# A mixture of experts on one core: two more slots in the ring of weights, shorter routing, small last loads, combines in halves

## The reference, cut to what matters

```
g_logits = t @ rg_w + rg_b                 # 4 groups
g_w      = softmax(g_logits)[argmax]
e_logits = (t @ re_w + re_b) of that group # 8 experts in a group
top_v, top_i = top_k(e_logits, 2)
weights  = g_w * softmax(top_v)
y[token] = sum over its 2 experts e of
           weights[e] * ((silu(t @ wg[e]) * (t @ wu[e])) @ wd[e])   # hidden width 512
h = h + y
return rmsnorm(h, final_norm_w)
```

## Time and profile before

| | |
|---|---|
| median of three runs | 1322.72 us (1322.7 to 1324.62) |
| the profiled execution, its own time | 1325.48 us |
| its span, first to last instruction | 1323.6 us |
| TensorE busy | 1281.5 us (97%) |
| VectorE, ScalarE busy | 588.7 us (44%), 470.3 us (36%) |
| DMA | 349.35 MB |
| chain that ended last | TensorE 83%, VectorE 6%, DMA 6%, ScalarE 3% |
| TensorE clock granted | 0.996 of full speed |

### The profile page before, as it was taken

One profiled execution on the slowest core, in us unless ns is written; L12 is line 12 of the kernel. 1 busy time (PEld: TensorE's weight loads), 2 busy tenths in 40 slices (PEclk: granted clock), 3 DMA queues, 4 the chain that ended last, 5 costly groups with the idle time before them and its releaser, 6 DMA issues.

```text
span 1323.6 us, 19228 instructions
## 1 busy us (share of the span) xinstructions
PE 1281.5 (97%) x8372; PEld 969.0 (73%) x8372; DVE 588.7 (44%) x939; ACT 470.3 (36%) x698; POOL 64.8 (5%) x68
## 2 busy tenths in 40 slices
PE   8999999999999999999999999999999999999996
PEld 7887888999998889979999998834344343443432
DVE  3576656444556576595555566522011110111112
ACT  4543555434454644544654554311111010110102
POOL 4021000000001021010200000000000000000000
PEclk9999999999999999999999999999999999999999
DMA  9776336555543534443455559489999999999995
GB/s 354 276 279 241 149 128 236 181 189 191 174 157 111 185 128 159 148 163 128 107 170 179 176 187 379 165 358 420 421 419 421 421 421 421 420 421 421 421 421 210
DMA packets 102548, 349.35 MB, mean 264 GB/s; under 512 B 6114, under 2 KB 9472, under 8 KB 77888
## 3 DMA queue, kind: packets, MB, share of 16 engines
q1 hardware_dynamic: 100912, 345.56, 68.5%
q0 software_dynamic: 1376, 2.50, 0.8%
q10 hardware_dynamic: 176, 0.07, 0.0%
HBM read 347.05 MB, written 1.05 MB: 263 GB/s over the span
## 4 chain that ended last, share of the span: by engine, by line
PE 83%; DVE 6%; DMA 6%; ACT 3%; issue 1%; DVEq 0%; ACTq 0%
PE bank L553 43%; PE bank L939 14%; PE bank L974 7%; DMA weights<-in_expert_w_up 4%; PE bank L790 3%; PE bank L749 3%; PE bank L474 2%; DMA arena<-in_expert_w_up 2%; DVE WHL L1412 2%; PE bank L580 2%; PE bank L510 1%; ACT WHL L993 1%; PE bank L520 1%; PE bank L690 1%; PE bank L716 1%
## 5 line engine op out<-in xcount | busy, mean ns | idle before, releaser
L553 PE MATMUL bank<-XH,WHL 128*128 128x256 f32 x2928 | 541.2, 285 | 7.6 <-DVE WHL L1412 3.8
L553 PEld LDWEIGHTS bank<-XH,WHL 128*128 128x128 f32 x2928 | 462.6, 193 | 12.1 <-DVE WHL L1412 5.5
L553 PE MATMUL bank<-XL,WHL 128*128 128x256 f32 x1464 | 415.4, 284 | 0.0
L1412 DVE TENSOR_TENSOR WHL<-weights,WHL 128x1024 fp32r<-128x1024 f32 x223 | 282.7, 1284 | 211.8 <-ACT WHL L993 211.4
L993 ACT ACTIVATE WHL<-weights 128x1024 fp32r<-128x1024 f32 x223 | 231.9, 1054 | 213.5 <-PE bank L553 207.9
L553 PEld LDWEIGHTS bank<-XL,WHL 128*128 128x128 f32 x1464 | 282.7, 193 | 0.1
L939 PE MATMUL bank<-arena 128*64 128x512 f32 x512 | 142.2, 593 | 2.6 <-DMA arena<-in_expert_w_up 2.6
L939 PE MATMUL bank<-weights,arena 128*64 128x512 f32 x384 | 113.6, 593 | 5.2 <-DMA weights<-in_expert_w_up 5.1
L553 PE MATMUL bank<-WHL,XH 128*128 128x512 f32 x320 | 102.4, 394 | 4.1 <-DVE WHL L1412 4.1
L939 PEld LDWEIGHTS bank<-arena 128*64 128x64 f32 x512 | 45.3, 137 | 72.0 <-issue 67.1
L2113 DVE SCALAR_TENSOR_TENSOR chainm<-bank,small,chainm 128x512 f32<-128x512 f32 x16 | 12.0, 750 | 183.1 <-PE bank L939 183.1
(11 more groups left out here) (347 smaller groups left out, 1216.4 us busy)
## 6 DMA issues: line engine op xcount, KB each, us to landing
weights<-in_w_in SPq DMA_DIRECT2D x58, 1024.0 KB, 5.0
arena<-in_expert_w_gate SPq DMA_DIRECT2D x32, 1024.0 KB, 19.6
arena<-in_expert_w_up SPq DMA_DIRECT2D x32, 1024.0 KB, 22.8
arena<-in_expert_w_down SPq DMA_DIRECT2D x32, 1024.0 KB, 26.2
weights<-in_expert_w_up SPq DMA_DIRECT2D x24, 1024.0 KB, 24.7
weights<-in_expert_w_down SPq DMA_DIRECT2D x24, 1024.0 KB, 24.4
weights<-in_expert_w_gate SPq DMA_DIRECT2D x24, 1024.0 KB, 21.0
weights<-in_w_ada SPq DMA_DIRECT2D x22, 1024.0 KB, 7.4
```

The costliest lines, as they stand in the source:

```text
L553: ins = e.matmul(o, l, r, start=first, skip_group_check=True, stop=g.part == g.parts - 1 and k == g.kc - 1 and n == 2)
L1412: e.tensor_tensor(lo, unit_weights(g, u), hi, ALU.subtract).then_inc(S.w_lo, 1)
```

## The change

- **Ring of eighteen.** The arena gives nine slots instead of eight, eight of them at the ring's start. To make room, several small tensors leave the arena or share memory with others. An eighteenth slot is `hT`, the transposed rows, free when the logits are done.
- **One buffer in place of two** for `hp`, `hpT`, `yo` and `wpick`; their writers wait for the readers in the pair before. `wpT`, the turned weights, keeps two.
- **Routing.** The picks of the first two pairs come from one 1024-wide product (`direct`) and one sum. `inpair` is made after the first choosing. ScalarE copies the token rows once more in chunk order (`full`), and the subtraction for `ulo` reads that copy. 15 spins instead of 32.
- **Order in a pair.** `turn_weights` stands between gate and up from the second pair on. Half of the combine comes before the transposes, the other half after them (and after the choosing). In the last pair the whole combine of the pair before comes between gate and up.
- **Last loads.** The second down half of the last pair is loaded as four pieces of 512 KB in place of two of 1,024 KB. VectorE's copy of the output waits for 6 of 8 signals.
- **Last norm.** Its weight row is kept in three pieces (`frow`), loaded after the first block's final norm. The products for the second half of a row are two, and VectorE's order at the end is changed.
- Three semaphores are merged into others.

```
-        c32 = sb("c32", [P, KC, 32])
+        spare = sb("spare", [P, 3 * T])
...
-        assert b5.at <= ARENA - 8 * SLOT, b5.at
+        wpick = maskf[:, HID:HID + T].rearrange("p (j s) -> p j s", j=TT)
+        assert b5.at <= ARENA - 9 * SLOT, b5.at
+        frow = [spare[:, 0:512], spare[:, 512:768], maskf[:, 768:1024]]
...
-        hp = [chainm[:, i * HID:(i + 1) * HID] for i in range(2)]
-        hpT = [maskf[:, i * HID:(i + 1) * HID].rearrange("p (k s) -> p k s", k=4) for i in range(2)]
+        hp = chainm[:, 0:HID]
+        hpT = maskf[:, 0:HID].rearrange("p (k s) -> p k s", k=4)
...
+            def turn_weights(p):
+                clear(6)
+                w.wait_ge(S.m_slots, weighed(p))
+                for j in range(TT):
+                    ins = e.transpose(bank[6][:, j * P:(j + 1) * P], wpick[:, j, :], ident[:, :])
+                ins.then_inc(S.m_wt, 1)
+                free[6] = (S.m_wc, p + 1)
+
-            def combine(p):
+            def combine(p, parts=range(4)):
                 w.wait_ge(S.m_wc, p + 1)
-                for i in range(4):
+                for i in parts:
...
-            spin(7, 32)
+            spin(7, 15)
...
                     free[b] = (S.m_h2 if wi else S.m_h1, p + 1)
+                    if wi == 0 and p:
+                        turn_weights(p)
+                        if p == NPAIR - 1:
+                            combine(p - 1)
...
-                if p:
-                    combine(p - 1)
+                if p == 0:
+                    turn_weights(0)
+                elif p < NPAIR - 1:
+                    combine(p - 1, (0, 1))
                 clear(7)
                 w.wait_ge(S.m_h2, p + 1)
...
                     choose(p // 2 + 1)
+                if 0 < p < NPAIR - 1:
+                    combine(p - 1, (2, 3))
                 w.wait_ge(S.m_hc, p + 1)
...
-                            x = moe_load(p, 2, half, s_)
+                            alone = p == NPAIR - 1 and k == 3
+                            x = 12 * NPAIR + s_ if alone else moe_load(p, 2, half, s_)
...
+            for j in range(TT):
+                e.activation(by_chunk(full)[:, j, :, :], xtok2[:, j, :].rearrange("p (q k) -> p q k", k=KC),
+                             ACT.Copy).then_inc(S.rn, 1)
...
-                w.wait_ge(S.rn, j + 1)
-                e.tensor_tensor(ulo[:, j, :].rearrange("p (k q) -> p k q", k=KC),
-                                xtok2[:, j, :].rearrange("p (q k) -> p k q", k=KC),
-                                uhi[:, j, :].bitcast(F32).rearrange("p (k q) -> p k q", k=KC),
-                                ALU.subtract).then_inc(S.rl, 1)
+                w.wait_ge(S.rn, TT + j + 1)
+                e.tensor_tensor(ulo[:, j, :], full[:, j, :], uhi[:, j, :].bitcast(F32), ALU.subtract).then_inc(S.rl, 1)
...
-            then(e.tensor_tensor(inpair, ph.unsqueeze(2).broadcast_to([P, two, 2, CAP]),
-                                 par.unsqueeze(3).broadcast_to([P, two, 2, CAP]), ALU.mult))
+            then(e.tensor_tensor(direct, ph.unsqueeze(2).broadcast_to([P, two, 4, CAP]),
+                                 dv[:, :, 0:4].unsqueeze(3).broadcast_to([P, two, 4, CAP]), ALU.mult))
             last()
-            for p in range(2):
-                slots_of(p, pick[:, :, p * P:(p + 1) * P], pair)
+            by_rank = direct.rearrange("p (j r) e s -> p j r (e s)", r=2)
+            e.tensor_tensor(pick[:, :, :], by_rank[:, :, 0, :], by_rank[:, :, 1, :], ALU.add).then_inc(S.m_slots, 1)
...
-                w.wait_ge(S.m_dn, 8 * p + 8)
-                if p >= 2:
-                    w.wait_ge(S.m_cb, 4 * (p - 1))
-                e.tensor_copy(yo[p % 2][0], bank[6][:, :]).then_inc(S.m_yv, 1)
+                w.wait_ge(S.m_dn, 8 * p + 6)
+                if p:
+                    w.wait_ge(S.m_cb, 4 * p)
+                e.tensor_copy(yo[0], bank[6][:, :]).then_inc(S.m_yv, 1)
...
+            w.wait_ge(S.fin, KC)
+            for f_, (c0, c1) in zip(frow, FROW):
+                e.dma_start(f_, a["norm_final_w_2"][c0:c1].rearrange("(o e) -> o e", o=1).partition_broadcast(P).rearrange(
+                    "p o e -> p (o e)")).then_inc(S.d_late, 16)
...
+                            if x >= 12 * NPAIR - 2:
+                                e.dma_start(moe_weights(x, 2, D)[:, 0, :], src[:, 2, :]).then_inc(moe_landed(x)[0], 16)
...
+            for s_ in range(2):
+                x = 12 * NPAIR + s_
+                w.wait_ge(*moe_released(x - len(moe_ring)))
+                e.dma_start(moe_weights(x, 2, D)[:, 0, :],
+                            a["expert_w_down_2"][0, NE - 2 + s_].rearrange("(p k) n -> p k n", p=P)[:, 3, :]).then_inc(
+                                moe_landed(x)[0], 16)
...
-        moe_ring = arena_ring[0:7] + [(base_slots[:, (nload + i) % RING, :], s_slot[(nload + i) % RING], None,
+        moe_ring = arena_ring[0:8] + [(base_slots[:, (nload + i) % RING, :], s_slot[(nload + i) % RING], None,
                                        (nload + i) % RING) for i in range(RING)]
-        moe_ring += arena_ring[7:] + [(late[:, i, :], sem(f"late_slot{i}_loaded"), (S.mm, len(units)), None) for i in range(2)]
+        moe_ring += arena_ring[8:] + [(late[:, i, :], sem(f"late_slot{i}_loaded"), (S.mm, len(units)), None) for i in range(2)]
+        moe_ring += [(hT[:, :, :].rearrange("p k t -> p (k t)"), sem("h_slot_loaded"), (S.lg, TT), None)]
```

More of the change, by code:

```diff
@@ L252, in build @@
         w8 = b5.take([P, KC])
-        frow = b5.take([P, D])
         tri = b5.take([P, P])
@@ L259, in build @@
         ss = b5.take([P, 8])
-        wpT = [hT[:, i, :] for i in range(2)]
+        wpT = [chainm[:, HID + i * T:HID + (i + 1) * T] for i in range(2)]
         rt = b5.take([P, TT, 96])
@@ L275, in build @@
         wcol = b5.take([P, TT, 1])
-        wpick = [hT[:, 2 + i, :].rearrange("p (j s) -> p j s", j=TT) for i in range(2)]
-        yhalf = b5.take([P, 512])
-        assert b5.at <= ARENA - 8 * SLOT, b5.at
+        wpick = maskf[:, HID:HID + T].rearrange("p (j s) -> p j s", j=TT)
+        assert b5.at <= ARENA - 9 * SLOT, b5.at
+        frow = [spare[:, 0:512], spare[:, 512:768], maskf[:, 768:1024]]
+        FROW = [(0, 512), (512, 768), (768, 1024)]
         b6 = Region(2048)
@@ L868, in tensor @@
             weave([gemm(n) for n in ("gk", "gv0", "gv1", "rq0", "rq1", "rk0", "rk1")],
-                  (2, gated(GL, [(S.gb, 1), by["gk"].freed[1]], by["gv1"].freed[1])), (13, gated_spread(GL, S.oGn)))
+                  (2, gated(GL, [(S.hb, 2), by["gk"].freed[1]], by["gv1"].freed[1])), (13, gated_spread(GL, S.oGn)))
             weave([gemm(n) for n in ("rv0", "rv1", "rv2", "rv3", "gg0", "gg1", "ma0", "ma1")],
@@ L971, in tensor @@
                         for s_ in range(2):
[L972 removed]
+                            alone = p == NPAIR - 1 and k == 3
+                            x = 12 * NPAIR + s_ if alone else moe_load(p, 2, half, s_)
                             w.wait_ge(*moe_landed(x))
[L974 to L975 removed]
+                            ins = e.matmul(bank[6 + n][64 * s_:64 * s_ + 64, :], hpT[:, k, 64 * s_:64 * s_ + 64],
+                                           moe_weights(x, 2, D)[:, 0 if alone else kk, n * 512:(n + 1) * 512],
+                                           start=k == 0, stop=k == 3)
                             if kk == 1:
@@ L1927, in vector @@
             weave([gemm(n) for n in ("gk", "gv0", "gv1", "rq0", "rq1", "rk0", "rk1")],
-                  (-1, log_decay()), (2, gated(GL, [(S.gb, 1), by["gk"].freed[1]])))
+                  (-1, log_decay()), (2, gated(GL, [(S.hb, 2), by["gk"].freed[1]])))
             for i in range(2):
@@ L2051, in vector @@
             chosen(0)
+            then(e.tensor_tensor(inpair, ph.unsqueeze(2).broadcast_to([P, two, 2, CAP]),
+                                 par.unsqueeze(3).broadcast_to([P, two, 2, CAP]), ALU.mult))
             then(e.tensor_tensor(eg, gl, gmax.broadcast_to([P, TT, 4]), ALU.subtract))
@@ L2105, in vector @@
                     assert nslots[0] == picked(p // 2 + 1)
-                if p >= 2:
-                    w.wait_ge(S.m_wt, p - 1)
-                slots_of(p, wpick[p % 2], wpair)
+                if p:
+                    w.wait_ge(S.m_wt, p)
+                slots_of(p, wpick, wpair)
                 assert nslots[0] == weighed(p)
@@ L2141, in scaled @@
                 w.wait_ge(S.rstd, NORMS + j + 1)
-                for n in range(2):
-                    c = slice(n * 512, (n + 1) * 512)
-                    e.scalar_tensor_tensor(out=normed[:, j, c], in0=xtok2[:, j, c], scalar=sj, in1=frow[:, c],
-                                           op0=ALU.mult, op1=ALU.mult).then_inc(S.t_out, 1)
             added(0, 0)
@@ L2150, in vector @@
             added(1, 1)
-            scaled(0)
+            inverted(0)
+            times_row(0, 0)
             summed(1)
-            scaled(1)
+            times_row(0, 1)
+            inverted(1)
+            times_row(1, 0)
```

(1 more changed line is left out.)

96 lines of the change are left out of this document (49 added, 47 removed).

## The result

The changed kernel takes 1312.1 us (median of six runs, 1311.37 to 1313.87) against 1322.94 us for the kernel before on the same chip: a ratio of 0.9918, with a 95% interval of 0.9906 to 0.993, or 9.3 to 12.4 us. Forecast were 1311.1 us, 11.65 us off the median. A second group of five runs gave 1313.38 against 1323.34 us, 0.9923 (0.9909 to 0.9936). The profiled execution took 1312.08 us with a span of 1310.4.

What follows compares the result with a forecast made beforehand. The stream of expert loads bounds the stage, TensorE what lies before and behind it. Savings of 3.84 + 4.99 + 1.97 + 0.80 + 0.05 = 11.65 us give 1311.1 us, range 1308.6 to 1314.8 us.

Steps and rivals of the forecast that it cites:

- What bounds: Expert stage: loads bound it; the time L, when the last up load frees TensorE, comes 8.83 us sooner.
- Shorter routing: Before the first choosing: 15 spins instead of 32, with VectorE's picks and subtractions in time, bring everything behind 3.84 us sooner.
- Rival (b): Routing: VectorE sets it, picks or subtractions up to 1.8 us late; 1312.9 us, chance 0.12.
- Eighteen slots: Load ring: two more loads issued before the hole leave 174 instead of 176 in the stream, saving 4.99 us.
- Rival (d): Load ring: the two extra loads don't shorten the stream, as something else holds its start or end; 1316.1 us, chance 0.06.
- The last pair: Last pair of experts: turning and combine moved between gate and up; down starts 1.97 us sooner against L.
- The end: After the last down phase: the final combine no longer waits for the first output half's copy, saving 0.8 us.
- The last norm: Final norm on VectorE: products split, VectorE's wait for ScalarE's root now under a product; 0.05 us saved.
- Rival (e): Last four 512 KB loads land late, the last 8.6 us after it is wanted; 1319.7 us, chance 0.05.
- Rival (c): Last pair: TensorE's clock falls after standing still, costing about 1.7 us; 1312.8 us, chance 0.08.
- Other pairs: Ordinary pairs: halved combines make TensorE 5 us quicker in sum, which gives nothing while the loads bound.
- Rival (f): Ordinary pairs: waits from single buffers make TensorE the bound; 1333 us at 2 us a pair, chance 0.05.

Runs made afterwards that it cites:

- the strided variant: Changed kernel with the routing's two subtractions reading the rows with a stride again, as in the kernel before: 1312.78 us.
- the variant in pieces: Changed kernel with the last pair's early combine split: two products between gate and up, one behind up, one behind the transposes; 1310.36 us.
- more work: Changed kernel with four more spins ahead of the transposes in each of the first fifteen pairs: 1319.58 us.
- whole combines: Changed kernel with the whole combine behind up, ahead of the transposes, in the ordinary pairs; last pair as changed: 1314.1 us.

## Why the prediction was right

**What bounds.** Right. S to G shortened by 8.8 us where 8.83 were forecast, and it answers one for one: 3.80 us for 17 spins, 4.95 us for two slots. It answers to the releases as a whole, not to the first alone: brought forward by 0.5 us by itself, the first gave nothing or 0.1 us.

**Shorter routing.** 3.84 forecast; the spins took 7.23 before and 3.43 after, 3.80. The picks stood 3.09 us behind S and the spins ended 3.43 behind it, a margin of 0.34 us where 0.15 was reckoned: product 1.22, sum 0.69, subtractions 2.35 for two. Rival (b) is out by this trace; the strided variant shows its size, 1.0 us for the subtractions alone. The change's parts depend on each other here: fewer spins pay in full only because the subtractions are quick enough. That the picks' shorter form is needed too is argued from the margin; no run has the old one.

**Eighteen slots.** 4.99 forecast, 4.95 measured. Rival (d) is out.

**The last pair.** Down starts 16.79 us behind G. L is G + 9.99 - 0.04, so that is L + 6.84, forecast L + 6.64. The term mis-sized is the second gate half, counted at 3.43: from G to the turning it took 3.65, and so up ended at L + 4.57, forecast L + 4.37. The saving was 1.8 instead of 1.97 us. The gap that the early combine fills is shorter than the combine, as forecast, and the variant in pieces shows what that cost: 0.8 us.

**The end.** The bare copy: 0.8 forecast, 0.8 measured by its own variant. The last norm: from the last combine's end 6.36 us before (1317.24 to 1323.6) and 6.22 after, 0.14 shorter where 0.05 was taken; no run has it alone.

**The small loads.** Rival (e) is out: undone, nothing changes either way. The half loads bring nothing here, and cost nothing that the time shows; with 2 us or more between the forecast landing and the need, a small cost would stay hidden. The rule of one MiB per DMA for full bandwidth in the Trainium skill, DMA: Bandwidth & Descriptors (Rules for kernel authors), is neither borne out nor refuted by 400 GB/s with small loads beside 421 and 404 with whole ones.

**The clock.** Rival (c) did not come: 0.88 and 0.69 us of standing still, and down took 7.09 us as always. The variant without spins shows that 3.15 us at once do bring it.

**Other pairs, the step that failed.** The prediction had the halves make TensorE 5 us quicker than before, hence 7.8 us to spare. Two pairs took 55.73 us against 55.80, so 0.5 us in all. The halves did save what they should, 0.76 us in two pairs against whole combines. What the prediction put at nothing is the turning's new place between gate and up: gate and up take 6.87 + 7.02 instead of 13.73, and the combine, now right behind up, 3.63 instead of 3.44, together 0.35 us a pair or 0.70 in two, which is all but what the halves save. TensorE had 4.8 us to spare, by the variants with more work and with whole combines and by its pace. It changed nothing in the time, but it sets what a next step can bring: at most 4.8 us from more slots or an earlier start, then TensorE is the bound. Rival (f) did not come: two pairs took no longer than before. The single buffers were not undone in a run of their own.

The medians give 10.8 and 10.0 us where the landmarks give 11.6; their intervals (9.3 to 12.4, 8.5 to 12.0) hold both. That the landmarks meet the forecast within 0.1 us is in part luck: the last pair gave 0.16 us less than forecast and the last norm 0.09 more.

## What to carry to other kernels

Where a stream of loads is full from its first release to its end, the end moves one for one with the releases as a whole and by one load's time for each load placed ahead of them (here: two loads, two load times). Look then for what TensorE waits for or spins through before that release. But count what the other engine has to spare, for it becomes the bound after that much. Work moved into a wait is free only as far as it is shorter than the wait. And where runs differ by 2 us or more before the change's place, measure from a landmark behind it.

## What the runs showed of the hardware

On TensorE the same products cost about 0.2 us more right behind those of gate, up or down than behind others: half a combine took 1.91 us behind up and 1.72 behind the transposes, a whole one 3.63 behind up (whole combines), 3.68 behind down, and 3.44 behind the turning. Taking up apart from gate, with the turning between them, made the two 6.87 + 7.02 = 13.89 us instead of 13.73. Why is not shown.

In the variant without spins the span ended 5.6 us behind the last product on VectorE instead of 2.1. The window before 1311 us is empty, the stores are done, and then the DMA engines move something once more (columns as above):

```profile
1311.00:1311.50 0.50, 0.00 (x0) 0.00 (x0) 0.00 (x0) 0.00 (x0) 0.00 (x0) 0.50 0.25 49
```

Its instruction queue moved 19 packets instead of the changed kernel's 18, so that this is a load of instructions may be guessed; but the variants with pieces and with more work also have 19 and no such tail. What the end waited for is open.
